# Hybrid decoder layer on one core: out-projection by column halves, earlier expert loads, residual rows on VectorE, overflow chain in parts

## The chip, the core and the metric

One core of a Trainium2 chip runs the whole layer in one launch. The metric is device microseconds from start to end of one execution. TensorE (PE) multiplies matrices into the eight PSUM banks of 512 fp32 columns, VectorE (DVE) and ScalarE (ACT) read those banks, GpSimd (POOL) works in SBUF and issues indirect DMAs, SyncE (SP) only issues DMAs. Each engine takes its own instructions in order and waits on counters that others raise.

## The reference, cut to what matters

512 tokens of width 1024, fp32 throughout. Each token row goes through one attention and convolution block, an output projection with a layer norm, and 2 of 32 experts.

```python
mix = jnp.concatenate([attn, conv], axis=-1) @ w_out[l]
x = _layer_norm(DEEPNORM_ALPHA * x + gate1 * mix, ln1_g[l], ln1_b[l])
h2 = (x * (1.0 + scale2) + shift2).reshape(bsz * seq, d)
...
group_logits = hf @ w_rg + b_rg          # 4 groups, top 1
exp_logits = (hf @ w_re + b_re)          # 8 experts in the group, top 2
...
hid = silu(h @ w_gate[e]) * (h @ w_up[e])    # 1024 -> 256
y = y + combine[:, e] * (hid @ w_down[e])    # 256 -> 1024
...
x = _layer_norm(DEEPNORM_ALPHA * x + gate2 * moe, ln2_g[l], ln2_b[l])
```

## The kernel before

**Tiling.** The tokens stand in TC = 4 tiles of 128 rows (0 to 3). Until about 222 us the kernel computes the six modulation rows, the input projection, attention and convolution; the change leaves that alone. `mixT` then holds the concatenated result, channel-major.

**Out-projection (PE, `project_out`, L1467).** For each tile, both column halves of 512 are computed one after the other, 8 steps of k each, into banks 4 to 7. An fp32 matmul shows as two in the trace, so a tile is 32 of them. `wo` (4 MB) comes in one DMA into SBUF from PAIR2. Between the tiles stand `spread_row` (a ones matmul that copies a modulation row to all partitions; rows 0, 1 are gate1, 2, 3 and 4, 5 the second modulation's shift and scale, 6, 7 gate2), `transpose_h2` (tile i of the modulated rows h2, turned for the router) and `route` (router logits). ACT copies each spread row out of its bank (`row_out`) and each turned tile (`h2T`).

**Layer norm (DVE, L1003 on).** For each tile: two halves of gate1 times the bank, ALPHA x plus that, statistics; then `moments`, a subtract-and-scale into `h2nat`, a wait for `rstd` from POOL (`inv_std`, a power of minus one half), and `h2p`, the tile of h2. ACT stores `h2p` to `h2_dram`, normalises `xs` in place (`normal`), and stores it to `x1_dram` once the residual rows are done. Those are x times g1r plus b1r (`x1_rows` on POOL for tiles 0 to 2, two VectorE instructions for tile 3, counted by `x1_last`).

**Routing.** DVE turns the logits into slots: `choose`, one-hot tables, PE multiplies them (`slot_table(1, ...)`), `slots_of` gives `slot_tok`. POOL then issues `gather(0)`, an indirect DMA of the 128 rows of h2 that experts pair 0 works on, and later `gather(1)`, `gather(2)`. DVE goes on with tile 3's residual rows, the combine weights `wk`, and the overflow chain: where tokens beyond 64 of one expert go. This ends in tables `colhot_ov`, `rowhot` (`hot_done`) for a second slot table and `blk_exp`, the experts of overflow blocks. `flag` holds the number of overflow blocks; with zero, the loops after `If(more > 0)` do not run.

**Experts.** 16 pairs of experts, 64 slots each. `pair(j)` on PE: `gates` (gate and up weights, counter `gu_done`), `turn`, `expert_rows` (turn the gathered rows of the next pair), `finish` (down weights, `dn_done`). The weights are 3 MB an expert: gate, up and down of 1 MB each. They stand in rings: `w_gu`, 8 slots of 2 MB, and `w_dn`, 6 slots of 1 MB.

**SP's queue** fixes the order of the loads by hand. A ring slot can only be loaded when what lay in its place is done: slots 0 and 1 need the modulation rows spread (`row_done` 6; w_dn[1] lies over gate2's row, so it needs rows 6, 7 spread), slots 2 and 3 need attention done, slots 4 and 5 lie where `wo` and the h2 buffers are, slot 6 over `mixT`, slot 7 over `xs`, whose tiles must be stored (`st_x1`). From expert 8 on, `load_gu(n)` waits for `gu_done` n - 7, and `load_dn(n)` for `dn_done` n - 5. So SP stands in line behind each wait:

```python
sp.wait_ge(out_done, 2 * TC)
load_gu(4); load_dn(4); load_gu(6)
# st_x1[0], st_x1[1]:  load_gu_part(7, 0)
# logit_done TC:       load_gu(5)
# st_h2:               load_dn(5)
# row_done 8, gathered[0]:  load_dn(1)
# st_x1[2], st_x1[3]:  load_gu_part(7, 1)
load_gu(GU_RING)       # expert 8, waits for gu_done 1
```

**Tail.** After the last pair the scattered expert outputs and x1 are loaded back, combined and normalised. The change does not touch its work.

## Time and profile before

| | |
|---|---|
| median of 3 runs | 563.89 us (563.58 to 564.46) |
| the profiled execution's own time | 564.14 us |
| its span in the trace | 562.4 us |
| PE busy | 512.1 us (91%) |
| DVE busy | 283.0 us (50%) |
| POOL busy | 110.7 us (20%) |
| ACT busy | 102.9 us (18%) |
| chain that ended last | PE 70%, DMA 14%, DVE 9%, SP's queue 3% |
| HBM traffic | 160.65 MB read, 18.35 MB written |

Times in the trace count from the span's start. The time of an execution is some 1.7 us longer than its span. Busy time of PE is modelled for pipelined matmuls and says little alone; the stretches and the chain of waits say where an engine stood still. A load's time "to landing" counts from its issue, with all that stands in the DMA rings ahead of it.

### The profile page before, as it was taken

The page shows a single profiled execution, that of the slowest core. Times are in us where ns is not written, and L with a number is a line of the kernel's source. Part 1 is how long each engine was busy: PE and PEld are TensorE (multiplying, and loading weights), DVE is VectorE, ACT ScalarE, POOL GpSimd, SP SyncE. Part 2 cuts the span into 40 slices and gives each one's busy share as a digit, 9 for nine tenths or more (in the row PEclk, how much of TensorE's full clock was granted, in tenths as well). Part 3 has the DMA queues.
Part 4 walks back from the last instruction along what each step waited for, and adds up shares of the span by engine and source line. Part 5 has one row for each costly group of instructions (what it writes and reads, how often), then busy time and mean ns, then how long its engine had stood idle before and what let it go on. Part 6 is the DMA issues. An engine that isn't in the chain of part 4 may idle for free.

```text
span 562.4 us, 6411 instructions
## 1 busy us (share of the span) xinstructions
PE 512.1 (91%) x2486; PEld 273.3 (49%) x2486; DVE 283.0 (50%) x519; ACT 102.9 (18%) x170; POOL 110.7 (20%) x115
## 2 busy tenths in 40 slices
PE   3999999999999999999983799999998799899873
PEld 2445468644445444444571455555554355444431
DVE  4765999655854573097568332322322123133378
ACT  1000211333132312001131211111111111221010
POOL 2000000143133310057512011111111111210015
PEclk9989999999999999999976799999999999989998
DMA  8999679943640173099479999999999999999953
GB/s 259 359 362 349 213 244 315 304 154 134 225 150 21 54 273 113 0 401 408 200 291 422 366 406 411 418 415 416 415 416 417 415 413 419 416 417 417 376 228 149
DMA packets 70815, 171.30 MB, mean 305 GB/s; under 512 B 7950, under 2 KB 45890, under 8 KB 62592
## 3 DMA queue, kind: packets, MB, share of 16 engines
q1 hardware_dynamic: 63552, 153.27, 71.8%
q10 hardware_dynamic: 2768, 9.49, 4.4%
q0 software_dynamic: 4464, 8.12, 3.8%
q8 instruction: 20, 0.33, 0.2%
q14 instruction: 11, 0.09, 0.0%
HBM read 160.65 MB, written 18.35 MB: 318 GB/s over the span
## 4 chain that ended last, share of the span: by engine, by line
PE 70%; DMA 14%; DVE 9%; SPq 3%; issue 2%; ACT 1%; POOL 0%; DVEq 0%; POOLq 0%; ACTq 0%
PE ps L1554 15%; PE ps L1428 11%; PE ps L1475 10%; DMA w_gu<-in_w_up_dram 8%; PE ps L1339 8%; PE ps L1563 7%; PE ps L1398 5%; PE ps L1545 2%; PE ps L1391 2%; SPq L436 2%; DMA y_tok<-y_dram 2%; PE ps L1493 2%; PE ps L1417 2%; DMA xg<-h_dram,slot_tok 2%; DVE x_back L1282 2%
## 5 line engine op out<-in xcount | busy, mean ns | idle before, releaser
L1554 PE MATMUL ps<-w_gu,xT 128*64 128x256 f32 x1024 | 118.7, 385 | 3.6 <-DMA w_gu<-in_w_up_dram 1.8
L1554 PEld LDWEIGHTS ps<-w_gu,xT 128*64 128x64 f32 x1024 | 72.0, 138 | 40.2 <-issue 3.3
L1428 PE MATMUL ps<-hT,w_stage 128*128 128x512 f32 x192 | 84.8, 595 | 0.0
L1198 DVE TENSOR_TENSOR ysb<-ps,rows_gate 64x512 f32<-64x512 f32 x64 | 44.1, 689 | 65.6 <-PE ps L1563 65.2
L1563 PE MATMUL ps<-w_dn,hidT 128*64 128x512 f32 x256 | 63.8, 620 | 6.1 <-issue 5.4
L901 DVE SCALAR_TENSOR_TENSOR acc_rows<-ada_stage,csil,acc_rows 128x256 f32<-128x256 f32 x112 | 55.2, 493 | 4.0
L1189 DVE TENSOR_TENSOR hid<-ps,silu_sb 128x128 f32<-128x128 f32 x32 | 9.3, 291 | 94.7 <-ACT silu_sb L815 94.7
L1475 PE MATMUL ps<-wo,mixT 128*128 128x512 f32 x128 | 55.6, 592 | 0.0
L1428 PEld LDWEIGHTS ps<-hT,w_stage 128*128 128x128 f32 x192 | 35.5, 190 | 41.0 <-issue 41.0
L1339 PE MATMUL ps<-hT,w_first 128*128 128x512 f32 x96 | 46.3, 629 | 0.9 <-DVE hT L927 0.9
L602 POOL DMA_INDIRECT y_dram<-ysb,slot_row x15 | 15.2, 1010 | 149.2 <-DVE ysb L1198 149.2
L1475 PEld LDWEIGHTS ps<-wo,mixT 128*128 128x128 f32 x128 | 24.2, 190 | 29.7 <-issue 29.7
L1563 PEld LDWEIGHTS ps<-w_dn,hidT 128*64 128x64 f32 x256 | 17.1, 138 | 30.3 <-issue 25.9
L815 ACT ACTIVATE silu_sb<-ps 128x128 f32<-128x128 f32 x32 | 8.9, 278 | 114.8 <-PE ps L1554 114.8
L1339 PEld LDWEIGHTS ps<-hT,w_first 128*128 128x128 f32 x96 | 18.3, 200 | 20.3 <-issue 20.3
L1398 PE MATMUL ps<-w_stage,hT 128*128 128x256 f32 x128 | 27.8, 379 | 0.0
L949 DVE TENSOR_TENSOR_SCAN stay<-stay,block_end 128x1280 f32<-128x1280 f32 x8 | 24.1, 3015 | 4.5 <-POOL stay L561 4.5
L1398 PEld LDWEIGHTS ps<-w_stage,hT 128*128 128x128 f32 x128 | 24.3, 190 | 3.7 <-issue 0.5
L1545 PE MATMUL ps<-ident,xg 128*128 128x128 f32 x128 | 19.3, 296 | 7.4 <-DMA xg<-h_dram,slot_tok 7.4
L596 POOL DMA_INDIRECT xg<-h_dram,slot_tok x16 | 16.6, 1035 | 48.0 <-PE ps L1554 24.0
L558 POOL TENSOR_SCALAR_AFFINE_SELECT stay<-stay 128x384 f32<-128x384 f32 x8 | 5.3, 659 | 100.5 <-ACT stay L701 100.5
L913 DVE SCALAR_TENSOR_TENSOR acc_cols<-ada_in,csil,acc_cols 128x512 f32<-128x512 f32 (+1 forms) x35 | 22.6, 645 | 1.5 <-DMA ada_in<-in_w_ada_dram 0.2
(211 smaller groups left out, 502.0 us busy)
## 6 DMA issues: line engine op xcount, KB each, us to landing
w_gu<-in_w_gate_dram SPq DMA_DIRECT2D x32, 1024.0 KB, 19.7
w_gu<-in_w_up_dram SPq DMA_DIRECT2D x32, 1024.0 KB, 22.7
w_dn<-in_w_down_dram SPq DMA_DIRECT2D x32, 1024.0 KB, 24.6
ada_stage<-in_w_ada_dram SPq DMA_DIRECT2D x16, 1024.0 KB, 6.0
w_stage<-in_w_in_dram SPq DMA_DIRECT2D x9, 1024.0 KB, 8.0
ada_in<-in_w_ada_dram SPq DMA_DIRECT2D x12, 512.0 KB, 9.4
y_dram<-zeros ACTq DMA_DIRECT2D x4, 1024.0 KB, 5.8
wo<-in_w_out_dram SPq DMA_DIRECT2D x1, 4096.0 KB, 15.3
```

The costliest lines, as they stand in the source:

```text
L596: g.indirect_dma_start(out=buf[:], out_offset=None, in_=h2_dram, in_offset=bass.IndirectOffsetOnAxis(ap=slot_tok[:, j:j + 1], axis=0), bou ...
L901: link(w.scalar_tensor_tensor(out=acc, in0=st[:, k], scalar=csil[:, 3, k:k + 1], in1=acc, op0=ALU.mult, op1=ALU.add))
L913: ins = w.scalar_tensor_tensor(out=acc, in0=ada_in[c][:, k], scalar=csil[:, 3, k:k + 1], in1=acc, op0=ALU.mult, op1=ALU.add)
L949: w.tensor_tensor_scan(out=st[:, 0:ZW][:, ::-1], data0=st[:, 0:ZW][:, ::-1], data1=block_end[:, ::-1], initial=1.0, op0=ALU.mult, op1=ALU. ...
L1198: ins = w.tensor_tensor(to[e * HD:(e + 1) * HD, b * 512:(b + 1) * 512], ps[b * HD:(b + 1) * HD, 6 + e, :], gate2r[b * HD:(b + 1) * HD, b * ...
L1339: ins = t.matmul(ps[:, n], w_first[:, k, n * P:(n + 1) * P], hT[:, k], start=k == 0, stop=k == KC - 1)
L1398: ins = t.matmul(dst[:, 0:CW], hT[:, k, i * P:(i + 1) * P], st[:, k], start=k == 0, stop=k == KC - 1)
L1428: ins = t.matmul(ps[:, 6], st[:, k, (f % 2) * P:(f % 2 + 1) * P], hT[:, k], start=k == 0, stop=k == KC - 1)
L1475: ins = t.matmul(ps[:, 4 + 2 * (i % 2) + n], mixT[:, k, i * P:(i + 1) * P], wo[:, k, n * 512:(n + 1) * 512], start=k == 0, stop=k == KC - 1)
L1545: ins = t.transpose(flat[:, k * P:(k + 1) * P], by_channel(xg[rows_buffer(j)])[:, k], ident[:])
L1554: ins = t.matmul(ps[a * SLOTS:(a + 1) * SLOTS, 2 + e, 0:2 * P], rows_in[:, k, e * SLOTS:(e + 1) * SLOTS], weights[:, :, k, a * P:(a + 1) * ...
L1563: ins = t.matmul(ps[b * SLOTS:(b + 1) * SLOTS, 6 + e, :], hidT[e][:, a * SLOTS:(a + 1) * SLOTS], weights[:, a, b * 512:(b + 1) * 512], sta ...
```

## The change

1. **Out-projection by halves.** `wo` becomes two buffers with two loads. PE computes the first half of all four tiles, then the second halves. DVE takes a half with `mix_half(i, n)`; the first halves of tiles 0 and 1 come ahead of its work on the a2 and b2 rows. `bn` gets a place for each tile.
2. **Earlier loads.** `load_gu(4)` waits for the first four halves instead of all eight. ACT moves gate2's row out of the way of w_dn[1] (`gate2_moved`), so that `load_dn(1)` comes before experts 2 and 3. Row 6 is spread between `route(1)` and `route(2)`, row 7 after the slot table.
3. **Residual rows.** Tile 2's go from POOL to DVE, beside tile 3's, after the slot table. Both tiles' x1 stores come after that on ACT. On POOL, the `inv_std_shift` of tile 2 stands ahead of tile 1's rows.
4. **Overflow chain in parts.** `overflow_hot` runs after the first `hidden`, `overflow_experts` after the second; SP waits for `flag_ready` 2.

PE from the spread rows on, before and after (`rows_gate_107` is gate2r, `wo_92` and `wo_93` the halves):

```order
L1461 MATMUL ps<-acc_rows,ones 128x512 x4
L1475 MATMUL ps<-wo,mixT 128x512 x16
L1461 MATMUL ps<-acc_rows,ones 128x512 x2
L1475 MATMUL ps<-wo,mixT 128x512 x16
L1486 MATMUL ps<-ident,h2p_99 128x128 x8
L1475 MATMUL ps<-wo,mixT 128x512 x16
L1493 MATMUL ps<-w_r,h2T 128x40 x8
L1486 MATMUL ps<-ident,h2p_100 128x128 x8
L1475 MATMUL ps<-wo,mixT 128x512 x16
```

```order
L1491 MATMUL ps<-acc_rows,ones 128x512 x4
L1502 MATMUL ps<-wo_92,mixT 128x512 x16
L1491 MATMUL ps<-acc_rows,ones 128x512 x2
L1502 MATMUL ps<-wo_92,mixT 128x512 x16
L1502 MATMUL ps<-wo_93,mixT 128x512 x16
L1513 MATMUL ps<-ident,h2p_100 128x128 x8
L1502 MATMUL ps<-wo_93,mixT 128x512 x8
L1520 MATMUL ps<-w_r,h2T 128x40 x8
L1513 MATMUL ps<-ident,h2p_101 128x128 x8
L1502 MATMUL ps<-wo_93,mixT 128x512 x8
L1513 MATMUL ps<-ident,h2p_100 128x128 x8
L1520 MATMUL ps<-w_r,h2T 128x40 x8
```

The 16-row groups now go by half; the first transposition follows six halves, not four.

SP's queue from the first expert on, before and after, with what each waits for (`w_gu_49` is slot 0 of its ring, `w_dn_57` of its own):

```order
L436 DMA w_gu_50<-in_w_gate_dram 128x2048
L436 DMA w_gu_50<-in_w_up_dram 128x2048
L436 DMA w_gu_51<-in_w_gate_dram 128x2048 [waits conv_ev,av_done]
L436 DMA w_gu_51<-in_w_up_dram 128x2048
L447 DMA w_dn_59<-in_w_down_dram 128x2x1024
L436 DMA w_gu_52<-in_w_gate_dram 128x2048
L436 DMA w_gu_52<-in_w_up_dram 128x2048
L447 DMA w_dn_60<-in_w_down_dram 128x2x1024
L436 DMA w_gu_53<-in_w_gate_dram 128x2048 [waits out_done]
```

```order
L440 DMA w_gu_50<-in_w_gate_dram 128x2048
L440 DMA w_gu_50<-in_w_up_dram 128x2048
L451 DMA w_dn_58<-in_w_down_dram 128x2x1024 [waits gate2_moved]
L440 DMA w_gu_51<-in_w_gate_dram 128x2048 [waits conv_ev,av_done]
L440 DMA w_gu_51<-in_w_up_dram 128x2048
L451 DMA w_dn_59<-in_w_down_dram 128x2x1024
L440 DMA w_gu_52<-in_w_gate_dram 128x2048
L440 DMA w_gu_52<-in_w_up_dram 128x2048
L451 DMA w_dn_60<-in_w_down_dram 128x2x1024
L440 DMA w_gu_53<-in_w_gate_dram 128x2048 [waits out_done]
L440 DMA w_gu_53<-in_w_up_dram 128x2048
L451 DMA w_dn_61<-in_w_down_dram 128x2x1024 [waits out_done]
```

`w_dn_58`, slot 1, now stands ahead of `w_gu_51`. It stood behind `w_dn_62` with a wait for `gathered0`; `w_gu_53`, slot 4, has a wait of its own, with a lower count.

DVE after the slot table, before and after:

```order
L1097 TENSOR_SCALAR slot_tok<-slot_row 128x16
L1121 TENSOR_TENSOR xs<-xs,g1r 128x1024
L1123 TENSOR_TENSOR xs<-xs,b1r 128x1024
L1127 TENSOR_REDUCE sc<-g_180 128x4
L1129 SCALAR_TENSOR_TENSOR sc<-sc 128x4
```

```order
L1115 TENSOR_SCALAR slot_tok<-slot_row 128x16
L1140 TENSOR_TENSOR xs<-xs,g1r 128x1024 x2
L1143 TENSOR_TENSOR xs<-xs,b1r 128x1024 x2
L1147 TENSOR_REDUCE sc<-g_181 128x4
L1149 SCALAR_TENSOR_TENSOR sc<-sc 128x4
```

Tile 2's two instructions stand in front of the combine weights and of the rest of the overflow chain. The diff, cut:

```diff
--- before.py
+++ after.py
...
         b24 = at("b24", [P, CW], PAIR1 + 47 * KB)
-        wo = at("wo", [P, KC, D], PAIR2)
+        wo = [at(f"wo{n}", [P, KC, 512], PAIR2 + n * 16 * KB) for n in range(2)]
         prob = [at(f"prob{n}", [P, ZW], PAIR2 + 32 * KB + n * 5 * KB) for n in range(2)]
...
             sp.wait_ge(zeroed, 16 * 4)
-            sp.dma_start(wo[:], w_out[0].rearrange("(k p) n -> p k n", p=P)).then_inc(ld_wo, 16)
+            for n in range(2):
+                sp.dma_start(wo[n][:], w_out[0].rearrange("(k p) n -> p k n", p=P)[:, :, n * 512:(n + 1) * 512]
+                             ).then_inc(ld_wo[n], 16)
             def load_gu_part(n, g):
...
             load_gu(1)
+            sp.wait_ge(gate2_moved, 1)
+            load_dn(1)
             sp.wait_ge(av_done, NH // 2)
...
                 load_dn(n)
+            sp.wait_ge(out_done, TC)
+            load_gu(4)
             sp.wait_ge(out_done, 2 * TC)
-            load_gu(4)
             load_dn(4)
...
             load_dn(5)
-            sp.wait_ge(row_done, 8)
             sp.wait_ge(gathered[0], 16)
-            load_dn(1)
             for i in (2, 3):
...
             load_dn(NE - 1)
-            sp.wait_ge(flag_ready, 1)
+            sp.wait_ge(flag_ready, 2)
             more = sp.value_load(flag[0:1, 0:1], min_val=0, max_val=NOVB)
...
                 g.tensor_tensor(shift_n[:, n:n + 1], neg_mean[:, n:n + 1], rstd[:, n:n + 1], ALU.mult).then_inc(shift_done, 1)
-            for i in range(TC):
-                inv_std_shift(i)
-                if i < TC - 1:
-                    x1_rows(i)
+            inv_std_shift(0)
+            x1_rows(0)
+            inv_std_shift(1)
+            inv_std_shift(2)
+            x1_rows(1)
+            inv_std_shift(3)
             pool.wait_ge(mixg_done, 2 * TC)
...
             gather(0, xg[0], gathered[0])
-            pool.wait_ge(x1_done, TC - 1)
-            pool.wait_ge(x1_last, 1)
+            pool.wait_ge(x1_done, TC - 2)
+            pool.wait_ge(x1_last, 2)
             g.memset(xg[1][:], 0.0).then_inc(xg_clear, 1)
...
             act.wait_ge(conv_done, len(CONV_OUT))
-            for r in range(6):
+            for r in range(4):
                 row_out(r)
+            act.wait_ge(ada_done, len(COLS) + NADACH - ADA1)
+            s.copy(gate2r[:], acc_rows[:, 3 * D:4 * D]).then_inc(gate2_moved, 1)
+            for r in range(4, 6):
+                row_out(r)
             def store_h2(i):
...
                 s.copy(h2T.rearrange("p k t -> p (k t)"), flat[:, 0:D]).then_inc(h2t_ev, 1)
+            row_out(6)
             act.wait_ge(h2_done, TC + 1)
...
             normal(TC - 1)
-            act.wait_ge(x1_done, TC - 1)
-            store_x1(TC - 2)
             act.wait_ge(gap_done, 1)
...
             s.activation(sc[:, 2, 0], sc[:, 1, 0], ACT.Exp).then_inc(gap_exp, 1)
-            row_out(6)
-            act.wait_ge(x1_last, 2)
-            store_x1(TC - 1)
             row_out(7)
+            for i in (3, 2):
+                act.wait_ge(x1_last, 6 - i)
+                store_x1(i)
             def xe_copy(j):
...
                     ada(i)
+            def mix_half(i, n):
+                q, cols = n * TC + i, slice(n * 512, (n + 1) * 512)
+                dve.wait_ge(out_done, q + 1)
+                w.tensor_tensor(h2nat[:, cols], ps[:, 4 + q % 4], gate1r[:, cols], ALU.mult).then_inc(mixg_done, 1)
+                dve.wait_ge(mixg_done, q + 1)
+                link(w.scalar_tensor_tensor(out=xs[:, i, cols], in0=xs[:, i, cols], scalar=ALPHA,
+                                            in1=h2nat[:, cols], op0=ALU.mult, op1=ALU.add))
+                did(w.bn_stats(bn[:, i, n], xs[:, i, cols]))
+            dve.wait_ge(row_ev, 2)
+            dve.wait_ge(probt_done, NH)
+            mix_half(0, 0)
+            mix_half(1, 0)
             dve.wait_ge(row_ev, 6)
...
             dve.wait_ge(ld_b1, 16)
-            dve.wait_ge(probt_done, NH)
             link(w.tensor_scalar(a2r[:], a2r[:], 1.0, None, ALU.add))
...
             w.engine_nop().then_inc(rows_ready, 1)
+            mix_half(2, 0)
+            mix_half(3, 0)
             def moments(n):
                 settle()
-                link(w.bn_aggr(mv[:, n], bn[:]))
+                link(w.bn_aggr(mv[:, n], bn[:, n % TC]))
                 if n < TC + 2:
...
                 wait(dve, h2_done, i)
-                for n in range(2):
-                    cols = slice(n * 512, (n + 1) * 512)
-                    dve.wait_ge(out_done, 2 * i + n + 1)
-                    w.tensor_tensor(h2nat[:, cols], ps[:, 4 + 2 * (i % 2) + n], gate1r[:, cols], ALU.mult
-                                    ).then_inc(mixg_done, 1)
-                    dve.wait_ge(mixg_done, 2 * i + n + 1)
-                    link(w.scalar_tensor_tensor(out=xs[:, i, cols], in0=xs[:, i, cols], scalar=ALPHA,
-                                                in1=h2nat[:, cols], op0=ALU.mult, op1=ALU.add))
-                    did(w.bn_stats(bn[:, n], xs[:, i, cols]))
+                mix_half(i, 1)
                 moments(i)
...
             dve.wait_ge(scaled, 2)
-            w.tensor_tensor(xs[:, TC - 1], xs[:, TC - 1], g1r[:], ALU.mult).then_inc(x1_last, 1)
-            dve.wait_ge(x1_last, 1)
-            w.tensor_tensor(xs[:, TC - 1], xs[:, TC - 1], b1r[:], ALU.add).then_inc(x1_last, 1)
+            for i in (3, 2):
+                w.tensor_tensor(xs[:, i], xs[:, i], g1r[:], ALU.mult).then_inc(x1_last, 1)
+            for i in (3, 2):
+                dve.wait_ge(x1_last, 4 - i)
+                w.tensor_tensor(xs[:, i], xs[:, i], b1r[:], ALU.add).then_inc(x1_last, 1)
             dve.wait_ge(gap_exp, 1)
...
             link(w.tensor_tensor(rowv, rowv, tmp, ALU.add))
-            for half in range(2):
-                b3 = oh_t[:].rearrange("p k c e -> p (k c) e")
-                link(w.tensor_tensor(b3, incl.unsqueeze(1).to_broadcast([P, 8, NE]),
-                                     iota[:, 8 * half:8 * half + 8].unsqueeze(2).to_broadcast([P, 8, NE]), ALU.is_le))
-                link(w.tensor_reduce(sc[:, 15 + half].rearrange("p k c -> p (k c)"), b3, AX, ALU.add))
-            link(w.tensor_scalar(blk_exp[:], sc[:, 15:17].rearrange("p n k c -> p (n k c)"), float(NE - 1), None, ALU.min))
-            column_hot(colhot_ov, colo, NOVP)
-            settle()
-            row_hot(rowv).then_inc(hot_done, 1)
+            def overflow_hot():
+                column_hot(colhot_ov, colo, NOVP)
+                settle()
+                row_hot(rowv).then_inc(hot_done, 1)
+            def overflow_experts():
+                for half in range(2):
+                    b3 = oh_t[:].rearrange("p k c e -> p (k c) e")
+                    link(w.tensor_tensor(b3, incl.unsqueeze(1).to_broadcast([P, 8, NE]),
+                                         iota[:, 8 * half:8 * half + 8].unsqueeze(2).to_broadcast([P, 8, NE]), ALU.is_le))
+                    link(w.tensor_reduce(sc[:, 15 + half].rearrange("p k c -> p (k c)"), b3, AX, ALU.add))
+                link(w.tensor_scalar(blk_exp[:], sc[:, 15:17].rearrange("p n k c -> p (n k c)"), float(NE - 1), None, ALU.min))
+                w.engine_nop().then_inc(flag_ready, 1)
             def overflow_slots():
...
                     y_out(2 * j - 1, 1)
+                if j == 0:
+                    overflow_hot()
                 hidden(2 * j + 1, 1)
...
                     overflow_slots()
+                    overflow_experts()
                 y_out(2 * j, 0)
...
             def spread_row(r):
-                t.matmul(ps[:, ROW_BANK[r]], ones[:], acc_rows[:, r * 512:(r + 1) * 512], start=True, stop=True
-                         ).then_inc(row_done, 1)
+                src = acc_rows[:, r * 512:(r + 1) * 512] if r < 6 else gate2r[:, (r - 6) * 512:(r - 5) * 512]
+                t.matmul(ps[:, ROW_BANK[r]], ones[:], src, start=True, stop=True).then_inc(row_done, 1)
             for r in range(4):
                 spread_row(r)
-            def project_out(i):
-                if i == 1:
-                    pe.wait_ge(av_ev, NH // 2)
-                    pe.wait_ge(conv_ev, len(CONV_OUT))
-                if i >= 2:
-                    pe.wait_ge(mixg_done, 2 * (i - 1))
-                for n in range(2):
-                    for k in range(KC):
-                        ins = t.matmul(ps[:, 4 + 2 * (i % 2) + n], mixT[:, k, i * P:(i + 1) * P],
-                                       wo[:, k, n * 512:(n + 1) * 512], start=k == 0, stop=k == KC - 1)
-                    ins.then_inc(out_done, 1)
+            def project_out(i, n):
+                q = n * TC + i
+                pe.wait_ge(ld_wo[n], 16)
+                if q >= 4:
+                    pe.wait_ge(mixg_done, q - 3)
+                for k in range(KC):
+                    ins = t.matmul(ps[:, 4 + q % 4], mixT[:, k, i * P:(i + 1) * P], wo[n][:, k],
+                                   start=k == 0, stop=k == KC - 1)
+                ins.then_inc(out_done, 1)
             def transpose_h2(i, halves=1):
...
                 ins.then_inc(logit_done, 1)
-            pe.wait_ge(ld_wo, 16)
             pe.wait_ge(ld_wr, 32)
...
             pe.wait_ge(conv_ev, len(CONV_OUT))
-            project_out(0)
+            project_out(0, 0)
+            project_out(1, 0)
             for r in (4, 5):
...
                 spread_row(r)
-            project_out(1)
+            project_out(2, 0)
+            project_out(3, 0)
+            project_out(0, 1)
+            project_out(1, 1)
             transpose_h2(0)
-            project_out(2)
+            project_out(2, 1)
             route(0)
             transpose_h2(1)
-            project_out(3)
+            project_out(3, 1)
             transpose_h2(2)
             route(1)
+            pe.wait_ge(gate2_moved, 1)
+            pe.wait_ge(mixg_done, 2 * TC - 1)
+            spread_row(6)
             route(2)
...
             slot_table(1, ps[:, 4, 0:3 * NPAIR], colhot)
-            pe.wait_ge(ada_done, len(COLS) + NADACH - ADA1)
-            for r in (6, 7):
-                spread_row(r)
+            spread_row(7)
             def expert_rows(j, sem_done, sem_half=None):
...
```

## Rows read from the trace of the kernel before

**Rows 1.** The page's 40 slices of 14.06 us: DMA busy tenths, GB/s.
```profile
DMA  8999679943640173099479999999999999999953
GB/s 259 359 362 349 213 244 315 304 154 134 225 150 21 54 273 113 0 401 408 200 291 422 366 406 411 418 415 416 415 416 417 415 413 419 416 417 417 376 228 149
```

**Rows 2.** Stretches: length, busy time of each engine, granted clock, DMA share, GB/s.
```profile
275.00:280.00 5.00, 5.00 (x13) 2.21 (x12) 2.08 (x3) 0.00 (x0) 4.92 (x2) 1.00 0.30 120
280.00:285.00 5.00, 5.00 (x27) 3.24 (x25) 1.65 (x3) 0.00 (x0) 0.11 (x1) 1.00 0.10 23
340.00:420.00 80.00, 80.00 (x585) 43.29 (x583) 21.70 (x40) 13.14 (x32) 12.18 (x12) 1.00 1.02 417
318.70:509.80 191.10, 181.87 (x1277) 96.75 (x1277) 49.18 (x99) 32.26 (x76) 28.39 (x28) 0.98 1.02 414
```

**Rows 3.** SyncE's DMA issues in order: start, time at issue, what, how many.
```profile
238.18 0.33 SPq L436 DMA_DIRECT2D w_gu<-in_w_gate_dram  x1
...
283.28 0.33 SPq L436 DMA_DIRECT2D w_gu<-in_w_gate_dram  x1
...
297.87 15.09 SPq L447 DMA_DIRECT2D w_dn<-in_w_down_dram  x2
313.05 0.42 SPq L436 DMA_DIRECT2D w_gu<-in_w_up_dram  x1
318.67 0.34 SPq L436 DMA_DIRECT2D w_gu<-in_w_gate_dram  x1
```

**Rows 4.** The chain that ended last: start, how long, what.
```profile
222.70 13.73 PE ps L1475 x32
...
266.85 1.71 PE ps L1493 x16
...
303.30 9.22 DMA xg<-h_dram,slot_tok
...
487.32 22.49 DMA w_gu<-in_w_up_dram
...
509.85 3.67 PE ps L1554 x32
```

**Rows 5.** DMA issues, us to landing: all gathers; then those at 315.3, 273.1, 273.5, 291.4.
```profile
xg<-h_dram,slot_tok POOLq DMA_INDIRECT x16, 8.4
...
xg<-h_dram,slot_tok POOLq DMA_INDIRECT x1, 5.9
...
h_dram<-h2p ACTq DMA_DIRECT2D x1, 512.0 KB, 2.7
...
x_dram<-xs ACTq DMA_DIRECT2D x1, 512.0 KB, 3.5
...
x_dram<-xs ACTq DMA_DIRECT2D x1, 512.0 KB, 10.1
```

**Rows 6.** Timeline of TensorE and GpSimd: start, us, line, shape, [idle before <-releaser].
```profile
287.00 2.57 PE L1493 MATMUL ps<-w_r,h2T 128*128 128x40 f32 x16 [1.16 <-ACT h2T L779]
...
270.00 1.52 POOL L582 TENSOR_TENSOR rstd<-var_e,mh 128x1 f32<-128x1 f32 x1 [1.85 <-DVE var_e L1001]
...
274.81 2.35 POOL L588 TENSOR_TENSOR xs<-xs,g1r 128x1024 f32<-128x1024 f32 x1 [3.02 <-ACT xs L763]
277.24 2.87 POOL L590 TENSOR_TENSOR xs<-xs,b1r 128x1024 f32<-128x1024 f32 x1
...
303.30 1.38 POOL L596 DMA_INDIRECT xg<-h_dram,slot_tok  x1 [14.62 <-DVE slot_tok L1097]
```

**Rows 7.** One stretch after TensorE's idle 1.16 us; clock before DMA share.
```profile
288.00:289.00 1.00, 1.00 (x8) 1.00 (x7) 1.00 (x2) 0.00 (x0) 0.67 (x1) 0.60 0.99 410
```

**Rows 8.** Timeline of VectorE at tile 2's last half and after the slot table.
```profile
266.89 0.69 DVE L1008 TENSOR_TENSOR h2nat<-ps,rows_gate 128x512 f32<-128x512 f32 x1 [3.12 <-PE ps L1475]
...
302.29 1.22 DVE L1121 TENSOR_TENSOR xs<-xs,g1r 128x1024 f32<-128x1024 f32 x1
...
311.20 0.42 DVE L1169 TENSOR_TENSOR oh_t<-cum,iota 128x256 f32<-128x256 f32 x1
```

12 lines of the change are left out of this document (7 added, 5 removed).

## The prediction

> **What bounds the kernel now.** I read first the page's 40 slices [rows 1]. From the 24th slice (323 us on) to the 37th the DMA engines are full, at 406 to 419 GB/s. Ahead of that stand slices with room: the 17th (225 to 239 us) moves nothing, the 20th and 21st (267 to 295 us) 200 and 291 GB/s. The stretches make it exact [rows 2]: DMA is at 1.02 and 417 GB/s from 340 to 420 us, 414 GB/s over 318.7 to 509.8, but 0.30 in 275 to 280 and 0.10 in 280 to 285. TensorE shows 80.00 of 80 us busy in the expert stage, which is modelled and proves nothing. The chain decides [rows 4]: it runs into the load of the last gate and up weights (issued at 487.32, 22.49 us under way), and PE's last 32 matmuls start at 509.85, when that has landed. So the expert stage ends when its bytes have come in, and the tail behind it is not touched by the change.
>
> When does this stream begin? SP issues the first expert loads at 238.18, then stands until 283.28 for `out_done` 8 [rows 3]. Expert 8, the first load that needs a ring slot used before, goes out at 318.67, when PE has finished `gates(0)`. Everything issued from there on is the same in both kernels: gate and up of 24 experts and 26 down blocks, 48 + 26 = 74 loads of 1.049 MB. At 417 GB/s they alone need 74 x 1.049 / 0.417 = 186 us, and the gathers and scatters come on top. PE was busy 181.87 us in the 191.10 from there to the last load's landing [rows 2], its throttled matmuls included, so it has some 9 us to spare and DMA none.
>
> It follows that filling the hole at 275 to 284 with 3 MB is **not** worth 3.15 / 0.417 = 7.5 us by itself. The rings hold 22 MB, and what is loaded into them sooner only makes DMA wait sooner for the first freed slot. The price of the whole change is how much earlier `gates(0)` ends.
>
> **The stretch from the projection to gates(0).** Its chain is: tile 3's last half at 283.3, norm, transposes, router, slot table, `slot_tok` just ahead of DVE's instruction at 302.29 [rows 8], then `gather(0)`, issued at 303.30 and 9.22 us under way [rows 4]. PE starts on the gathered rows at 312.5, and `gates(0)` ends 6.15 us later, at 318.67.
>
> **1. The projection by halves.** Same matmuls, same spread rows between. PE's own time is unchanged, 13.73 us for each 32 [rows 4], if it never waits. Where could it? The second halves wait for `mixg_done` of a half three places earlier, which is long past. The first transposition now stands behind six halves, the second behind seven: 222.70 + 7 x 6.87 + 1.7 (two spread rows, four matmuls of the projection's shape, 4/32 of 13.73) + 1.71 for `route(0)` [rows 4] = 274.2 at the earliest, and a tile's transposes more. Tile 1's `h2p` must be there. On POOL, tile 0's rows now stand in front of its `rstd`. Tile 2 of before gives the offset: half taken by DVE at 266.89 [rows 8], rows begun by POOL at 274.81 and 2.35 + 2.87 us long [rows 6]. Tile 0's last half is done after five, at 222.70 + 34.3 + 1.7 = 258.7, so rows 266.6 to 271.8, `rstd` 1.52 [rows 6] to 273.3, one DVE instruction of 1024 columns (1.22 [rows 8]) to 274.5. So PE waits nothing or, at worst, about 1 us. I take 0. The first halves of tiles 0 and 1 fall in time when DVE only waited for the a2 row. Cover: 6.9 us of PE for each half against about 2.1 us of DVE (three instructions like the 0.69 us one [rows 8]).
>
> **2. Earlier loads.** dn(1) joins the first batch; its wait `gate2_moved` is one ACT copy, which ACT reaches while PE is still in the first halves, long before SP issues at 238.18, and nothing is held behind it. gu(4) is released after four halves, 222.70 + 27.5 + 1.7 = 251.9. Both run in the hole of [rows 2]. In the batch that starts at 283.3 there were gu4, dn4, gu6, half of gu7, gu5, dn5: 9 loads of 1.049 MB and two stores of 0.524 (h2 and x1): 10.49 MB, 25.2 us at 417 GB/s. The share 0.10 in 280 to 285 says that it began at 284.5, so it ran until 309.7, and the gather, issued at 303.30, had 6.4 us of work beside it. After: 7 loads and two stores, 8.39 MB, 20.1 us, until 304.6. One hole can open: half of gu7 waits for tile 1's x1, now stored at about 284 instead of 273.5. Landing took 3.5 us idle and 10.1 loaded [rows 5], so up to 294, with some 9 us of loads in front: 0 to 1.5 us. The stream ends at 304.6 to 306.
>
> **What the gather then takes.** Its price in an empty machine is not in the trace. Lower end: 1.38 us of POOL's issue [rows 6] and then 2.7, in which a 0.5 MB store of h2 landed at 273.1, when the machine was empty [rows 5]: 4.1. Upper end: 9.22, as now. Nearest row: the gather at 315.3, with two loads in the rings, 5.9 [rows 5]. With 1.3 to 2.7 us of stream left at its issue I take 5.2, between 4.1 and 5.9: **4.0 us gained**. All 16 gathers have a median of 8.4 [rows 5], while the loads around them are over 20 us under way (22.49 [rows 4]), so it is not the depth of the backlog that costs but that there is one. The Trainium skill ("DMA: Bandwidth & Descriptors", Queues, rings and completion order) says the same: each DMA engine takes turns between queue rows, one packet at a time. By that rule a shorter backlog that still outlasts the gather buys nothing; this is rival B.
>
> **3. Row 6 in front of route(2).** Before, PE stood 1.16 us for ACT's copy, and then `route(2)` took 2.57 us [rows 6] where `route(0)` took 1.71 [rows 4], because the granted clock fell to 0.60 in 288 to 289 [rows 7], that is from 2.4 to 1.2 GHz. Row 6 (two matmuls, 0.86 us) fits in the gap. If the clock holds, transposes and logits end earlier and DVE, with 2 us fewer to wait, has `slot_tok` up to 2 us sooner. But the gather then meets the stream that ends at 304.6 or later, so at most 1 us arrives. Bounds 0 and 1.0; I take 0.5, the middle, as nothing in the trace shows this gap filled. The Trainium skill ("TensorE: Matmul & The Clock Gate", Part 1) has the half rate as the rest state that activity lifts, which is for the filler.
>
> **4. Tile 2's rows on DVE.** Two instructions of 1.22 us [rows 8] behind `slot_tok`, so off the gather's path. They push the chain that ended at 311.2 [rows 8] to 313.7. `hidden(0)` is due when `gates(0)` has ended, 308.5 + 6.15 = 314.7, and ScalarE after it. Cost 0, with 1 us to spare; if all gains came together it would cost under 1 us. `overflow_hot` (a 1024-column instruction and three small ones, about 2 us) then lies beside PE's `gates(1)`, `overflow_experts` (four of 0.42 us [rows 8] and a small one, 2 us) beside `finish(0)` and `gates(2)`. POOL is rid of 5.2 us [rows 6]. `gather(1)` waits for two DVE multiplications (until 304.7), as long as before.
>
> **5. SP's queue behind the new x1 store.** Tile 2's x1 is stored at 307.3 instead of 291.4. SP waits for it before the second half of gu7, and expert 8 stands behind. It lands 3.5 us later in an empty machine [rows 5], at 311 to 312, and `gates(0)` ends near 314.2. Cost 0.
>
> **Sum.** `gates(0)` ends 4.0 + 0.5 = 4.5 us earlier. Does the stream start as much earlier? Before, two loads issued at 312.96 and 313.05 [rows 3] kept DMA busy to about 319.9, 1.2 us after expert 8's issue; after, the machine is empty and the first byte comes 1.2 us after the issue (283.28 to 284.5). The same. 564.14 - 4.5 = 559.6 for the profiled execution; its time is 0.25 above the median of the runs, 563.89, so **559.4 us**.
>
> **The rivals.**
> - **A, the forecast** (0.60): 558.0 to 561.0.
> - **B, the gather meets a stream that outlasts it** (0.14). It needs holes of 3 us or more, so that the backlog ends after 308. For: half of gu7 waits on a store that took 10.1 us loaded. Against: the 9 us of loads in front of it. The gather stays at 8 to 9.2 us: 562.7 to 563.9.
> - **C, the hole only moves** (0.08): PE waits up to 1 us at tile 1 or 2, the gather takes 5.9 to 7: 561 to 562.7.
> - **D, the clock holds and everything adds up** (0.11): gather 4.1, chain 1 to 1.5 sooner: 557.3.
> - **E, slower: the late x1 store holds expert 8** (0.07). If tile 2's store lands as it did loaded, 10.1 us after 307.3, SP issues gu7's half at 317.4 and expert 8 behind it. The stream begins at 318.6 with 2.5 us of gu7, so expert 8 begins at 321.1 instead of 319.9: 1.2 us slower, 565.1. It decides from a landing of 8.9 us on. Against: only gu7's half and small transfers are left then.
>
> That the loads do not come forward at all is excluded by the order of SP's queue, and by `out_done` 4 being due at 251.9.
>
> **The numbers.** A measurement of this kernel can tell about 0.2%, 1.1 us, so faster is below 562.8 and slower above 565.0. Faster holds A, C, D and a little of B: 0.81. Same holds the rest of B and those of E that stay under 565.0: 0.13. Slower: 0.06. The range reaches from D's 557.3 to 562.6, which leaves out B and E.
>
> **What would show it.** In the profile after: DMA share near 1 in 272 to 280 us; loads idle or thin between 305 and 315; the first gather 4 to 6 us to landing; PE's transposes of the gathered rows at 308 to 309 in place of 312.5; expert 8's load at 313.5 to 315; DMA full from there, and the last gate and up load landing 4 to 5 us sooner with the tail as long as before. `route(2)` near 1.7 us says the clock held. It would be wrong if the gather still took 8 us or more, if expert 8's issue came later than PE's end of `gates(0)`, or if PE showed a wait at a transposition before 283 us.

## Result, and the profile after

The changed kernel takes 561.42 us in the median of 7 runs (559.8 to 564.34), the kernel before, on the same chip, 564.93 (563.58 to 568.49): ratio 0.9937, 95% interval 0.9907 to 0.9966, so 1.9 to 5.3 us faster. The profiled execution took 561.42 us, its span is 559.7 (before 562.4).

The two profiled executions already differ by 1.04 us where the out-projection begins (first matmul at 222.54 before, 221.50 after). That is no part of the change: over the 14 profiles of this study this point lies between 220.66 and 222.85, in no order of edits. Below, **net** means against that point.

The page's 40 slices of the changed kernel, as [rows 1]:

```profile
DMA  8999679943641173099889699999999999999963
GB/s 263 359 363 351 228 241 315 307 159 122 234 143 27 49 260 128 0 393 421 349 319 400 251 386 418 415 418 415 418 414 417 415 414 418 416 417 416 379 238 151
```

The hole of slices 20 and 21 (200 and 291 GB/s) has gone up to 349 and 319, but slice 23 (308 to 322 us) fell from 366 to 251. Stretches of the changed kernel, columns as in [rows 2]:

```profile
275.00:280.00 5.00, 5.00 (x13) 2.13 (x13) 4.33 (x6) 1.01 (x1) 4.00 (x3) 1.00 0.57 231
280.00:285.00 5.00, 5.00 (x31) 3.61 (x29) 3.55 (x8) 1.69 (x2) 3.23 (x1) 1.00 0.63 190
...
300.00:305.00 5.00, 0.23 (x1) 0.00 (x0) 4.79 (x12) 0.59 (x1) 3.63 (x3) 0.50 1.01 404
305.00:310.00 5.00, 1.67 (x8) 1.57 (x8) 4.32 (x21) 0.52 (x1) 0.00 (x0) 0.50 0.78 310
310.00:315.00 5.00, 5.00 (x28) 2.75 (x28) 0.11 (x1) 1.94 (x3) 0.99 (x1) 0.55 0.57 211
315.00:320.00 5.00, 4.19 (x39) 2.53 (x37) 2.01 (x5) 0.54 (x2) 0.00 (x0) 1.00 0.71 252
320.00:330.00 10.00, 10.00 (x78) 5.27 (x76) 5.15 (x15) 2.08 (x5) 0.99 (x1) 1.00 1.01 412
```

The first two rows stand against 0.30 and 0.10 before. The hole has moved: 305 to 320 is now at 0.78, 0.57, 0.71, where the kernel before had 1.00, 0.82, 1.03. And the granted clock is 0.50 from 300 to 310 and 0.55 to 315, that is about 1.2 of 2.4 GHz. What TensorE did, from the timeline after:

```profile
274.84 7.03 PE L1502 MATMUL ps<-wo,mixT 128*128 128x512 f32 x16
...
284.29 1.10 PE L1491 MATMUL ps<-rows_gate,ones 128*128 128x512 f32 x2
285.62 1.98 PE L1520 MATMUL ps<-w_r,h2T 128*128 128x40 f32 x16 [0.22 <-ACT h2T L791]
...
308.33 1.97 PE L1576 MATMUL ps<-ident,xg 128*128 128x128 f32 x8 [8.10 <-DMA xg<-h_dram,slot_tok]
310.23 5.76 PE L1585 MATMUL ps<-w_gu,xT 128*64 128x256 f32 x32
316.80 0.33 PE L1603 MATMUL ps<-ident,hid 128*128 128x128 f32 x1 [0.81 <-DVE hid L1215]
317.06 3.67 PE L1585 MATMUL ps<-w_gu,xT 128*64 128x256 f32 x32
```

GpSimd's timeline has the first gather, and SP's the second half of gu7 and then expert 8:

```profile
300.10 1.38 POOL L601 DMA_INDIRECT xg<-h_dram,slot_tok  x1 [12.34 <-DVE slot_tok L1115]
```

```profile
311.01 0.33 SPq L440 DMA_DIRECT2D w_gu<-in_w_up_dram  x1
316.04 0.33 SPq L440 DMA_DIRECT2D w_gu<-in_w_gate_dram  x1
```

The gather goes out at 300.10 instead of 303.30 [rows 4], and PE starts on its rows at 308.33: 2.2 us net from the earlier issue and 1.0 from the gather itself (8.18 us against 9.22), 3.2 together. `gates(0)` then takes 5.76 us against 4.17, while the same 32 matmuls of `gates(1)` take 3.67. That gives 1.6 back. Expert 8 goes out at 316.04 against 318.67 [rows 3]: 2.63 us sooner, **1.6 net**. The last gates start at 507.58 against 509.85 [rows 4]: 1.2 net. The tail is as long as before (52.1 and 52.6 us to the end of the span; over the 14 profiles 51.4 to 52.7, and 54.2 in a0_after).

### The profile page after: what moved, and what is told of

Read it like the earlier page. It is cut to its first block, busy times and chain, and to the rows that moved or that the text cites. A ratio compares the mean times of both kernels' runs of the same rounds, so it can differ in the third digit from the quotient of the medians.

```text
span 559.7 us, 6415 instructions
## 1 busy us (share of the span) xinstructions
PE 509.1 (91%) x2486; PEld 271.7 (49%) x2486; DVE 286.8 (51%) x521; ACT 103.7 (19%) x171; POOL 106.7 (19%) x113
## 4 chain that ended last, share of the span: by engine, by line
PE 71%; DVE 10%; DMA 10%; SPq 4%; issue 3%; ACT 1%; POOL 1%; DVEq 0%; POOLq 0%
PE ps L1585 16%; PE ps L1457 11%; PE ps L1502 10%; PE ps L1368 8%; PE ps L1594 8%; PE ps L1427 5%; DMA w_gu<-in_w_up_dram 4%; PE ps L1576 3%; PE ps L1420 2%; SPq L440 2%; DMA y_tok<-y_dram 2%; PE ps L1446 2%; SPq L451 2%; DVE x_back L1311 2%; DMA xg<-h_dram,slot_tok 1%
## 5 line engine op out<-in xcount | busy, mean ns | idle before, releaser
L1585 PE MATMUL ps<-w_gu,xT 128*64 128x256 f32 x1024 | 122.3, 393 | 3.7 <-DMA w_gu<-in_w_up_dram 3.6
L1585 PEld LDWEIGHTS ps<-w_gu,xT 128*64 128x64 f32 x1024 | 73.7, 141 | 42.2 <-issue 4.8
L1594 PE MATMUL ps<-w_dn,hidT 128*64 128x512 f32 x256 | 61.9, 604 | 6.4 <-issue 5.7
L1576 PEld LDWEIGHTS ps<-ident,xg 128*128 128x128 f32 x128 | 16.1, 196 | 15.4 <-DMA xg<-h_dram,slot_tok 9.7
```

The lines of the kernel that those rows point to most:

```text
L1576: ins = t.transpose(flat[:, k * P:(k + 1) * P], by_channel(xg[rows_buffer(j)])[:, k], ident[:])
L1585: ins = t.matmul(ps[a * SLOTS:(a + 1) * SLOTS, 2 + e, 0:2 * P], rows_in[:, k, e * SLOTS:(e + 1) * SLOTS], weights[:, :, k, a * P:(a + 1) * ...
L1594: ins = t.matmul(ps[b * SLOTS:(b + 1) * SLOTS, 6 + e, :], hidT[e][:, a * SLOTS:(a + 1) * SLOTS], weights[:, a, b * 512:(b + 1) * 512], sta ...
```

## Experiments

Diffs are cut at `...`. Two numbers per run carry the verdicts beside the ratio: expert 8's issue and the start of the last gates, both from the first out-projection matmul on. The third and the fourth are the gather's time to landing and the time of `gates(0)`. The last is what DMA moved from 45 to 100 us after that matmul (before: 267.5 to 322.5 us), from the rows of its two stretches, GB/s by length.

| kernel | ratio to before, 95% | gather us | gates(0) us | expert 8 | last gates | MB, 45 to 100 |
|---|---|---|---|---|---|---|
| before | 1 | 9.22 | 4.17 | 96.1 | 287.3 | 17.48 |
| the change | 0.9937 [0.9907, 0.9966] | 8.18 | 5.76 | 94.5 | 286.1 | 18.13 |
| a0_after, the same again | 0.9949 [0.9927, 0.9972] | 8.24 | 5.54 | 94.4 | 285.8 | 18.23 |
| u1_loads | 0.9974 [0.9954, 0.9994] | 9.23 | 4.89 | 94.7 | 286.9 | 17.56 |
| u2_row6 | 0.9934 [0.9909, 0.9959] | 4.36 | 5.33 | 93.2 | 284.7 | 18.54 |
| b1_row6 | 0.9979 [0.9960, 0.9998] | 9.80 | 4.22 | 94.5 | 287.3 | 18.15 |
| u3_rows | 0.9959 [0.9936, 0.9983] | 4.90 | 5.00 | 95.2 | 286.4 | 17.87 |
| h1_hold | 0.9893 [0.9853, 0.9934] | 4.24 | 4.54 | 89.4 | 283.8 | 18.81 |
| w1_warm | 0.9901 [0.9868, 0.9934] | 7.50 | 3.67 | 91.2 | 283.3 | 19.07 |
| c1_both | 0.9890 [0.9849, 0.9930] | 3.9 | 3.67 | 87.7 | 283.5 | 18.93 |
| u4_overflow | 0.9928 [0.9903, 0.9953] | 8.15 | 5.58 | 94.3 | 286.2 | 18.15 |
| w2_row6 | 0.9912 [0.9889, 0.9934] | 5.3 | 3.67 | 91.3 | 283.4 | 19.36 |
| w3_dn5 | 0.9879 [0.9853, 0.9905] | 4.6 | 3.67 | 90.7 | 283.6 | 19.26 |
| b2_warm | 0.9976 [0.9958, 0.9994] | 9.00 | 3.67 | 96.0 | 288.3 | 17.38 |

Each chip had its own runs of the kernel before (564.7 to 565.8 us in the median). The ratios are of medians of few runs, with intervals of 0.4 to 0.8%; the traced columns come from one execution each.

**a0_after** is the changed kernel once more, with the first group.

> The change as it is, once more, beside the kernel before on this chip and as the yardstick of the next three. Both theories: 0.990 to 0.997 of before. The stretch from PE's first out-projection matmul to the end of gates(0) was 96.1 us before (222.54 to 318.67) and 94.5 after (221.50 to 316.04); it should repeat within 0.5 us. If the granted clock during gates(0) varies from run to run, the 5.76 us that gates(0) took will vary between 4.2 and 6.

It repeats: 1.7 us net for expert 8 and 1.5 for the last gates. Two profiles of one kernel differ by 0.2 us in either, so smaller differences below say nothing.

**u1_loads: the early loads undone**, the rest of the change kept.

```diff
-            sp.wait_ge(gate2_moved, 1)
-            load_dn(1)
...
-            sp.wait_ge(out_done, TC)
-            load_gu(4)
             sp.wait_ge(out_done, 2 * TC)
+            load_gu(4)
...
             sp.wait_ge(gathered[0], 16)
+            load_dn(1)
```

> The early loads alone undone: gate and up of expert 4 again behind all eight halves, the down block of expert 1 again behind gather 0. Theory G (what counts is the end of gates(0); the loads matter only by emptying the rings before the gather): slot_tok stays as early as in the change, the stream then lasts some 5 us longer, the first gather takes 9 us or more in place of 8.2, gates(0) ends 0.5 to 2 us later, and the time is 0.5 to 2 us over the change. Rival H (the 3 MB are worth their 7.5 us of DMA time): 6 to 8 us over the change. Rival N (they do nothing): within 0.3 us of it.

Ratio 0.9974 against 0.9949 on the same chip, intervals that overlap; last gates 1.0 us later than in a0_after. DMA is full from 305 to 320:

```profile
305.00:310.00 5.00, 0.93 (x5) 0.93 (x6) 4.16 (x20) 0.00 (x0) 0.00 (x0) 0.50 1.02 419
310.00:315.00 5.00, 5.00 (x31) 3.11 (x32) 0.00 (x0) 2.46 (x3) 0.99 (x1) 0.65 1.03 418
315.00:320.00 5.00, 4.20 (x39) 2.48 (x35) 2.01 (x5) 0.54 (x2) 0.00 (x0) 1.00 1.03 421
```

So 3 MB loaded early are worth about 1 us, not 7.5: they leave a hole behind them. Expert 8's issue is hardly later than with them (94.7 against 94.4 and 94.5), so the first theory had the size of the loss but not its place: it expected `gates(0)` to end 0.5 to 2 us later. What the loads gain there is the shorter gather, and the slower `gates(0)` (5.76 against 4.89) takes most of it back.

**u2_row6: row 6 again behind the slot table.**

```diff
...
             pe.wait_ge(gate2_moved, 1)
-            pe.wait_ge(mixg_done, 2 * TC - 1)
-            spread_row(6)
             route(2)
...
+            spread_row(6)
             spread_row(7)
```

> Row 6 again spread behind the slot table, so that PE stands still for 1.2 us in front of route(2). Theory C (the filler kept the granted clock up through the router): route(2) takes 2.5 us again instead of 1.98, slot_tok is 2 us later, but the stream's end holds the gather, so PE starts on it only 0.5 to 1.5 us later; the two rows behind the slot table bring the clock up sooner, so gates(0) takes 4.2 us and not 5.8. Net within 1 us of the change. Rival: the clock at gates(0) has nothing to do with it, gates(0) stays at 5.8, and the time is 1 to 2 us over the change.

`route(2)` is slow again and the gather is issued at 302.42, 2.9 us later net. TensorE's timeline, and GpSimd's:

```profile
285.09 3.61 PE L1520 MATMUL ps<-w_r,h2T 128*128 128x40 f32 x16 [1.25 <-ACT h2T L791]
...
306.83 1.97 PE L1575 MATMUL ps<-ident,xg 128*128 128x128 f32 x8 [2.57 <-DMA xg<-h_dram,slot_tok]
```

```profile
302.42 1.38 POOL L601 DMA_INDIRECT xg<-h_dram,slot_tok  x1 [15.28 <-DVE slot_tok L1115]
```

Yet PE starts on the rows at 306.83, 0.9 us net sooner than with the filler. The gather that went out later landed in 4.36 us. The stream had not quite ended: its last load (expert 5's down block, issued at 294.83) landed at 306.1, and the gather 0.7 us behind it, at 306.8. In the changed kernel that load landed at 308.6 and the gather at 308.3. Two to three microseconds of earlier `slot_tok` were worth nothing, or less. The first theory had the total, within 1 us of the change, but wanted PE's start 0.5 to 1.5 us later and `gates(0)` at 4.2 us, measured 5.33. The rival's 1 to 2 us more did not come.

**b1_row6: the kernel before, with row 6 spread in front of `route(2)` and nothing else.**

```diff
...
             route(1)
+            pe.wait_ge(ada_done, len(COLS) + NADACH - ADA1)
+            pe.wait_ge(mixg_done, 2 * TC - 1)
+            spread_row(6)
             route(2)
...
-            for r in (6, 7):
-                spread_row(r)
+            spread_row(7)
```

> The kernel before with nothing but row 6 moved in front of route(2). Theory C: slot_tok 2 us earlier, but with the longer stream of before (until about 310) the gather is not done sooner than 1 us; with gates(0) at the lower clock, as in the change, the time is within 0.5 us of before. Rival (the router's clock is what the change gained): 2 to 3 us under before.

The filler does what it should (`route(2)` 1.98 us), and the gather takes 9.80 us instead of 9.22. PE starts on the rows 1.7 us sooner net and expert 8 goes out 1.6 us sooner, but the last gates start no sooner. Ratio 0.9979, barely apart from 1.

**u3_rows: tile 2's residual rows on POOL.** Here both tiles' rows stand ahead of tile 3's `inv_std`; the kernel before had tile 2's alone there.

```diff
...
             inv_std_shift(2)
             x1_rows(1)
+            x1_rows(2)
             inv_std_shift(3)
...
-            for i in (3, 2):
-                w.tensor_tensor(xs[:, i], xs[:, i], g1r[:], ALU.mult).then_inc(x1_last, 1)
+            w.tensor_tensor(xs[:, TC - 1], xs[:, TC - 1], g1r[:], ALU.mult).then_inc(x1_last, 1)
```

> Tile 2's residual rows back on POOL and its x1 store back in front of the slot table; the rest as in the change. Its 0.5 MB then go through the DMA rings ahead of the first gather, 1.26 us at 417 GB/s. Theory G: the gather lands 0 to 1.3 us later, the time is 0 to 1.3 us over the change. Rival (VectorE's 2.4 us more, or the late store that SyncE waits for, cost something): 0.5 to 2 us under the change.

TensorE's timeline, at the transposes of tile 3:

```profile
290.82 1.94 PE L1513 MATMUL ps<-ident,h2p 128*128 128x128 f32 x8 [3.32 <-DVE h2p L1045]
```

PE waits 3.32 us for h2, which neither theory had, and the gather goes out at 304.73, 4.7 us later net. PE starts on the rows only 1.4 us later: again a short gather (4.90 us) gives back most of what was lost. At the last gates the move of tile 2's rows is worth 0.3 us, about as much as two profiles of one kernel differ, and the ratios overlap: a gain isn't shown.

**u4_overflow: the overflow chain in one piece** ahead of the first `hidden`, as before.

```diff
-            sp.wait_ge(flag_ready, 2)
+            sp.wait_ge(flag_ready, 1)
...
-                w.engine_nop().then_inc(flag_ready, 1)
+
+            overflow_experts()
+            overflow_hot()
...
-                if j == 0:
-                    overflow_hot()
...
-                    overflow_experts()
```

> The change with the overflow chain back in one piece, all of it ahead of the first hidden. In the changed kernel VectorE had 6.3 us between the end of that chain (310.1) and the first hidden (316.45), and the two parts moved take about 4 us. Theory (cover): nothing happens, ratio within 0.2% of the changed kernel's 0.994 to 0.995. Rival (the split carries part of the gain): expert 8's issue 1 us or more later, ratio 0.997.

VectorE's timeline, the end of the chain and the first `hidden`:

```profile
312.69 1.23 DVE L1106 TENSOR_TENSOR rowhot<-sc,iota 128x1024 bf16<-128x1024 f32 x1
316.05 0.29 DVE L1217 TENSOR_TENSOR hid<-ps,silu_sb 128x128 f32<-128x128 f32 x1 [2.14 <-ACT silu_sb L826]
```

It ends at 313.9 and VectorE still waits 2.14 us for ScalarE. The split carries nothing here.

**h1_hold: the second half of expert 5's gate and up, and its down block, behind the gather.**

```diff
-            load_gu(5)
+            load_gu_part(5, 0)
             for n in range(2):
                 sp.wait_ge(st_h2[n], 32)
-            load_dn(5)
             sp.wait_ge(gathered[0], 16)
+            load_gu_part(5, 1)
+            load_dn(5)
```

> The change, with the up half of expert 5's weights and its down block issued behind gather 0 instead of ahead of it: 2.1 MB less in the rings when the gather goes out. Theory G: the stream ends near 301, the gather takes 4.1 to 5.9 us instead of 8.2, gates(0) ends 2.5 to 4 us sooner; the held loads and the half of expert 7 run until about 313, and the time is 2 to 3.5 us under the change. Rival (DMA time is the bound and none may be lost): the hole costs up to 5 us of stream, and the time is 2 to 5 us over the change.

Two megabytes less in front of the gather, and it lands in 4.24 us. Expert 8 goes out 5.1 us sooner net than in the change, more than the 2.5 to 4 expected, and the last gates start 2.3 us sooner.

**w1_warm: six unused row matmuls** between row 7 and the gathered rows. They write a bank whose content is not read before it is written again, and no output uses them; b2_warm, c1_both, w2_row6 and w3_dn5 hold such matmuls too.

```diff
+            pe.wait_ge(row_ev, 7)
+            for _ in range(6):
+                t.matmul(ps[:, 6], ones[:], gate2r[:, 0:512], start=True, stop=True)
             pe.wait_ge(gathered[0], 16)
             expert_rows(0, xe_done, xe_half)
```

> The change, with 6 more row matmuls (6 fp32 matmuls of 512 columns, results unused) between the last spread row and the first gather, so that PE does not stand still. Theory W (the change lost part of its gain to the half clock in gates(0), 5.76 us against 4.17 before): the clock is at 1.00 through the first gathered rows and gates(0), they take 1.1 and 3.7 us instead of 1.97 and 5.76, gates(0) ends up to 3 us sooner and the time falls by 1.5 to 3 us. Rival (the stream of loads sets the end whatever PE does): under 0.5 us of difference.

TensorE's timeline, the unused matmuls, the transposes and `gates(0)`:

```profile
299.63 7.28 PE L1668 MATMUL ps<-rows_gate,ones 128*128 128x512 f32 x12
307.26 1.16 PE L1576 MATMUL ps<-ident,xg 128*128 128x128 f32 x8 [0.35 <-DMA xg<-h_dram,slot_tok]
308.65 3.67 PE L1585 MATMUL ps<-w_gu,xT 128*64 128x256 f32 x32 [0.23 <-ACT xT L851]
```

The transposes take 1.16 us instead of 1.97 and `gates(0)` 3.67 instead of 5.76: 2.9 us, and the last gates start 2.8 us sooner net than in the change. PE's start is 0.7 us sooner too (gather 7.50 us). The half clock was most of what the change had lost on the way. The ratio's interval overlaps with the change's; the traced columns carry this reading.

**c1_both: the hold and four unused matmuls.** The two edits above, with `range(4)`.

> Both together: the loads held back behind gather 0, and 4 of the extra row matmuls. If the two savings are independent, 3.5 to 6 us under the change. If the stream then becomes the bound (held loads and expert 7's half until about 313 while gates(0) ends at 309), the saving is that of the held loads alone plus at most 1 us: 2.5 to 4 us under the change.

Two stretches:

```profile
300.00:305.00 5.00, 5.00 (x11) 1.94 (x10) 4.93 (x8) 0.59 (x1) 3.17 (x3) 0.83 0.41 139
305.00:310.00 5.00, 4.72 (x40) 3.06 (x40) 4.31 (x22) 2.36 (x4) 1.44 (x2) 1.00 1.00 346
```

Expert 8 goes out at 87.7, 3.6 us sooner than with the matmuls alone, and the last gates start no sooner (283.5). The hold paid with a hole: DMA at 0.41 in 300 to 305. The loads held back stand in front of expert 8 afterwards.

That suggested to count bytes. From 13 us after the first matmul to 1 us before the last gates, DMA moves 106.2 to 106.8 MB in every kernel, and from 100 us on it is full. So what was moved by then says when the last load is in. This is bookkeeping, not a cause, and it gives the start of the last gates only where they wait for a load. Stretches of the kernel before:

```profile
235.54:267.54 32.00, 31.90 (x88) 14.84 (x86) 24.04 (x30) 4.55 (x5) 18.05 (x10) 1.00 0.89 360
267.54:287.54 20.00, 18.84 (x79) 11.07 (x78) 10.49 (x18) 3.27 (x3) 9.07 (x6) 1.00 0.47 188
287.54:322.54 35.00, 21.08 (x126) 14.87 (x127) 22.86 (x96) 8.08 (x13) 5.42 (x6) 0.66 0.98 392
322.54:508.85 186.31, 178.51 (x1252) 94.64 (x1248) 47.97 (x96) 31.47 (x73) 28.39 (x28) 0.98 1.02 415
```

The changed kernel, and below it w3_dn5:

```profile
266.50:286.50 20.00, 19.78 (x88) 11.91 (x86) 16.92 (x22) 5.01 (x6) 14.01 (x9) 1.00 0.81 306
286.50:321.50 35.00, 19.55 (x132) 12.93 (x132) 23.28 (x94) 7.66 (x13) 5.80 (x7) 0.71 0.87 343
321.50:506.58 185.08, 176.92 (x1239) 94.21 (x1238) 49.53 (x100) 31.14 (x72) 28.35 (x28) 0.98 1.02 414
```

```profile
267.85:287.85 20.00, 19.78 (x88) 11.92 (x87) 16.95 (x22) 5.01 (x6) 14.02 (x9) 1.00 0.81 312
287.85:322.85 35.00, 27.51 (x174) 16.67 (x175) 26.29 (x105) 8.85 (x15) 6.80 (x8) 0.85 0.97 372
322.85:505.48 182.63, 174.64 (x1210) 91.88 (x1205) 46.65 (x91) 29.91 (x70) 27.42 (x27) 0.97 1.02 415
```

The change moves 306 x 20 = 6.12 MB where the kernel before moved 3.76, gaining 2.36, and in the next 35 us it loses 1.71 of them. The rest, 0.65 MB, is 1.6 us at 415 GB/s; measured at the last gates 1.2. For w1_warm it is 1.59 MB, 3.8 us; measured 4.0. In 12 of the 13 other rows of the table this sum and the measured start of the last gates agree within 0.8 us; b1_row6 is 1.6 off. About half of that is in its trace: the last gates do not wait for a load there. Their own had landed at 508.2, and PE came to them 0.8 us later, from its work ahead of them. TensorE's timeline of b1_row6, and for comparison of the kernel before:

```profile
487.52 4.34 PE L1603 MATMUL ps<-norm,ones_back 1*128 1x512 f32 x8
...
495.81 4.46 PE L1556 MATMUL ps<-w_gu,xT 128*64 128x256 f32 x32
...
509.00 3.67 PE L1556 MATMUL ps<-w_gu,xT 128*64 128x256 f32 x32
```

```profile
489.12 3.77 PE L1601 MATMUL ps<-norm,ones_back 1*128 1x512 f32 x8
...
496.60 3.67 PE L1554 MATMUL ps<-w_gu,xT 128*64 128x256 f32 x32
...
509.85 3.67 PE L1554 MATMUL ps<-w_gu,xT 128*64 128x256 f32 x32 [0.78 <-DMA w_gu<-in_w_up_dram]
```

The granted clock is 0.56 from 490 to 495 and 0.76 to 500 in b1_row6, 0.80 and 0.86 in the kernel before. b2_warm (0.50, 0.84) and w2_row6 start their last gates without a wait for a load too.

The last three kernels ran with this account in mind.

**w2_row6: w1_warm with row 6 behind the slot table.** The two diffs together.

> The six unused row matmuls before the gather, with row 6 back behind the slot table. Alone the one gave the last gates 283.3 us after the first out-projection matmul, the other 284.7, the changed kernel 286.1. Theory by bytes (between the projection and the last load's landing every kernel moves 106.3 MB, so only DMA's idle time counts): gates(0) takes 3.7 us, gather about 4.3 and the last gates come at 283 to 283.5, no sooner than with the matmuls alone, ratio 0.988 to 0.990. Rival (what both save adds up): 281.9, ratio 0.987 or below.

The saving doesn't add: 283.4. The gather landed after 5.3 us, at 306.2, but the unused matmuls ran until 307.4 and held PE. By bytes (19.36 MB) the last gates were due at 282.8. They start without a wait for a load, behind TensorE's own work, so here the two bounds have met. `route(2)` took 1.95 us here behind the same 1.25 us gap that left it at 3.61 in u2_row6: the clock fell later, at about 288 against 285 us. So the filler isn't always needed to hold it.

**w3_dn5: w1_warm with only expert 5's down block behind the gather.**

```diff
-            load_dn(5)
             sp.wait_ge(gathered[0], 16)
+            load_dn(5)
```

> The six unused row matmuls and only the fifth down block (1 MB) behind the gather, instead of 2 MB in the run with both. Theory by bytes: the hole is shorter, by 1 MB, and the gather lands in 5 to 6 us; last gates at 282.5 to 283.3 us after the first out-projection matmul, ratio 0.987 to 0.990. Rival (the backlog must be gone for the gather to be fast): gather 7 us or more, as in the run with the matmuls alone, and the same 283.3.

One megabyte was enough to bring the gather to 4.6 us, landed at 306.1. The unused matmuls ran on until the transposes at 308.54, so it could not show in PE's start. Ratio 0.9879, the lowest. The last gates, at 283.6, start no sooner than with the matmuls alone (283.3), and miss the 282.5 to 283.3 expected by bytes: in the traces this hold gains nothing on top.

**b2_warm: the kernel before with unused matmuls of the same columns.**

```diff
+            pe.wait_ge(row_ev, 7)
+            for _ in range(24):
+                t.matmul(ps[:, 6, 0:P], ones[:], ones[:], start=True, stop=True)
             pe.wait_ge(gathered[0], 16)
```

> The kernel before with unused matmuls of the same number of columns before the gathered rows, nothing else. There gates(0) took 4.17 us, against 5.76 in the changed kernel and 3.67 at full clock. Theory (the half clock before gates(0) is general, the kernel before just had less of it): transposes and gates 1 to 1.5 us shorter, ratio 0.997 to 0.998. Rival (the gain of the matmuls comes from something else, such as an earlier gather): ratio 0.993 or below. A third outcome, 1.00, would say that DMA in the kernel before has no idle time there to win back.

The ratio, 0.9976, is where the first theory put it, and the transposes (1.16 instead of 1.97) and `gates(0)` (3.67 instead of 4.17) are 1.3 us shorter, as it said. But the last gates start 1.0 us later than in the kernel before, so the traces don't carry the ratio. The gather was issued 1.05 us later net (`route(2)` at 3.64 us, against 2.57 in [rows 6], at a clock that falls a little sooner or later from run to run), expert 8 went out at 96.0, and at the end PE came later than the load (above). What the matmuls gain in the whole time of this kernel stays open; the half clock to win back here is 1.3 us, against 2.9 in the changed kernel.

## Why the prediction was right, and where it was not

The time, 561.4, lies in the range (557.3 to 562.6), but above the forecast's own band (558.0 to 561.0) and inside rival C's (561 to 562.7), whose mechanism did not come: PE waited at no tile, and the gather took longer than its 5.9 to 7. Of the signs of being right four failed: the gather (4 to 6 us, measured 8.18), expert 8's load (313.5 to 315, measured 316.04), a DMA share near 1 in 272 to 280 (0.57 from 275 on) and the last load 4 to 5 us sooner (2.3). One of the signs of being wrong came true: a gather of 8 us or more. The kernel before measured 1.04 us more beside it than the 563.89 that the forecast started from, so as a gain, 3.5 us of 4.5, the time fits the forecast better. But the mechanism behind it came only in part, and that the time hit is partly luck. The traced gain, 1.6 us net at expert 8, is a third of the 4.5 predicted; the median's 3.5 is larger than the traces' 1.2 to 1.5 at the last gates. So the traces stand between rivals B and C and the median nearer to the forecast. That difference stays open: the interval of the ratio begins at 1.9 us, and the start of the projection alone varies by 2.2 us from profile to profile.

- **What bounds the kernel: right.** DMA is full from 320 on, the tail is as long, and 3 MB in the hole were not worth 7.5 us (u1_loads). But "the price of the whole change is how much earlier `gates(0)` ends" holds only while nothing is owed: h1_hold and c1_both brought expert 8 forward by 5.1 and 6.9 us and the last gates by 2.3 and 2.6, since held loads then stood in front. Bytes moved by a fixed time is the better account. And TensorE's "9 us to spare" were not there at the end: in b1_row6, b2_warm and w2_row6 it is PE that comes last at the last gates.
- **1, the halves: right.** PE waits nowhere in the projection, and the last half starts at 274.84. Tile 1's `h2p` was done at 273.10, 1.4 us before the estimate (0.4 net). The halves themselves were not undone in any run.
- **2 and 3, gather and filler: the failed step.** In the whole change the term "gather 5.2, 4.0 us gained" measured 8.18, a gain of 1.04. With the 2.2 us of the earlier issue 3.2 of the 4.5 us reached PE's start. The cause is the overlap of the two steps. u2_row6, without the filler, starts on the rows 4.1 us net sooner than the kernel before, just what step 2 alone promised; with the filler it is 3.2. So the filler's +0.5 measured -0.9.
- **The stream's end, in the same step: mis-sized.** It was put at 304.6 to 306; the last load issued ahead of the gather landed at 308.6, with the gather (308.3). The same sum had put the end at 309.7 in the kernel before, where DMA still moved 412 GB/s up to the gather's landing at 312.5. The stream of 8.39 MB at 417 GB/s left out what went beside it. From 281.5 to 308.5 us DMA moved 382 GB/s, 10.3 MB, in the first 5 us only 287 GB/s: among them the gather itself and at least part of both x1 stores (1 MB, issued from 302.62, where step 5 had 307.3) and of `gather(1)` (0.5 MB, 303.31). What the stores and `gather(1)` cost the first gather was not separated by a run. The price at the lower bound was right: 4.1 predicted, 3.9 and 4.2 in c1_both and h1_hold, where no load was left in front.
- **3, the clock: right here.** It held (`route(2)` 1.98), and `slot_tok` came 3.2 us sooner, 2.2 net, a little above "up to 2". "At most 1 us arrives" was right for the changed kernel, while in the kernel before (b1_row6) 1.7 us arrived.
- **4, tile 2's rows and the overflow chain: cost 0, right.** The chain ended at 310.1, 6.3 us ahead of the first `hidden`; u4_overflow shows that the split gains nothing either. On POOL, in the order of u3_rows, the rows made PE wait 3.32 us, of which 0.3 us was left at the last gates.
- **5, the late x1 store: cost 0, right for SP's queue.** The stores went out at 302.6 and landed in 7.0 and 7.2 us, SP issued gu7's half at 311.01, and expert 8 waited for `gates(0)`. That they went beside the gather the prediction had not priced.
- **Missed: the clock in `gates(0)`.** No term or rival had it. PE stood for 8.10 us with the clock at 0.50, and its transposes and gates took 1.97 + 5.76 us instead of 1.16 + 3.67: 2.9 us. The kernel before lost 0.8 + 0.5 there, so of the 3.2 us that reached PE's start the clock took 1.6. So at expert 8: 4.1 from step 2, less 0.9 for the filler and 1.6 for the clock, 1.6 us net. With 4.17 in `gates(0)` on record in the trace of before, against 3.67 for the next, the question was there to be asked.

Rival B's mechanism (the gather meets a stream that outlasts it) came, by 0.3 us and without the hole of 3 us that B needed. The Trainium skill says that each DMA engine takes turns between queue rows by packet ("DMA: Bandwidth & Descriptors", Queues, rings and completion order). By that the gather pays as long as any backlog lasts, whatever its depth; the runs agree in the main. The gather took 8.15 to 9.8 us where the last load landed after it (four traces show that landing), 3.9 and 4.2 where no load was left in front, and where the stream ended under way it landed 0.3 to 0.7 us behind the last load (4.4, 4.6, 5.3 and 7.5 us in u2_row6, w3_dn5, w2_row6 and w1_warm; 1.6 us behind it, 4.9, in u3_rows). So a backlog that ends sooner does shorten it.

## What to carry to other kernels

Filling a hole in DMA's time moves it to where the rings are full and the first freed slot is late; count the megabytes moved by a fixed time in both kernels, not the hole alone. A small transfer on the critical path should not meet a backlog that is not yet needed: hold back just as many loads as it takes. 1 MB was enough for a gather of 4.6 us (w3_dn5), and 2 MB opened a hole of their own, with DMA at 0.41 (c1_both). Beside the unused matmuls neither hold moved the last gates; h1_hold alone did, by 2.3 us. And where TensorE waits several microseconds ahead of the work that frees the next buffers, look at the granted clock behind the wait.

Kernels that do so are clear of the kernel before: h1_hold, which only moves two loads, 0.9893 [0.9853, 0.9934], and w3_dn5 0.9879 [0.9853, 0.9905]. Their last gates start 2.3 and 2.5 us sooner than the change's; as ratios, h1_hold's interval overlaps with the change's [0.9907, 0.9966] and w3_dn5's just doesn't. The next one to try, w3_dn5 with four unused matmuls instead of six, was not run.

## What was not expected of the hardware

- **VectorE beside GpSimd.** The same instruction takes 1.31 us alone (tile 1) and 3.44 while GpSimd works on `xs` (tile 2). VectorE's timeline in the changed kernel, then GpSimd's:

```profile
271.79 1.31 DVE L1043 SCALAR_TENSOR_TENSOR h2p<-h2nat,rstd,rows_b 128x1024 f32<-128x1024 f32 x1 [0.45 <-POOL rstd L587]
...
277.57 3.44 DVE L1043 SCALAR_TENSOR_TENSOR h2p<-h2nat,rstd,rows_b 128x1024 f32<-128x1024 f32 x1 [0.61 <-POOL rstd L587]
```

```profile
277.59 2.34 POOL L593 TENSOR_TENSOR xs<-xs,g1r 128x1024 f32<-128x1024 f32 x1
280.01 3.23 POOL L595 TENSOR_TENSOR xs<-xs,b1r 128x1024 f32<-128x1024 f32 x1
```

  GpSimd's first instruction ends at 279.93; VectorE's ends at 281.01, 1.1 us after that; GpSimd's second, 0.55 us longer than the same instruction on tile 0 (2.68), ends 2.2 us later still. VectorE looks as if it stood until GpSimd's first was through; that GpSimd's second then stood is likely, not shown. The Trainium skill ("SBUF — State Buffer", SBUF: two separate sides) describes the port pair that the two share as an exclusive lock, by which the loser stands for the whole instruction; VectorE's row agrees. It cost PE nothing here.
- **The clock and unused work.** With unused matmuls in the wait the granted clock was back at 1.00 when `gates(0)` began, and it took 3.67 us. The Trainium skill ("TensorE: Matmul & The Clock Gate", Part 1) has the half rate as the rest state that activity lifts; the runs agree. In w1_warm the clock was 0.50 over the first unused matmuls, from 299.63 to 303.5 us, and 0.99 from there (12 in 7.28 us); in w2_row6, where the four matmuls of rows 6 and 7 stood ahead of them, it was at 1.00 from 302 us on, and the 12 took 5.31.
- **Later can be no worse.** A gather issued 2.9 us later landed 0.9 us sooner net (u2_row6): the last load in front landed sooner as well, 85.2 against 87.1 us after the first out-projection matmul.
